# Token projection of a decoder step on one core: the memory's part moved from last to second, and the tokens put back tile by tile

## The reference, cut to what matters

```python
IN_WIDTHS = (NSA_H * HD, 3 * NSA_H, 2 * NSA_G * HD, 2 * NSA_G * HD, 2 * NSA_G * HD,
             ML_W, ML_W, ML_H, ML_H, MEM_W, N_BRANCH * D_MODEL)
...
def split_proj(x, norm_mix, w_in):
    offs = [int(o) for o in np.cumsum(IN_WIDTHS)[:-1]]
    return jnp.split(rmsnorm(x, norm_mix) @ w_in, offs, axis=-1)
```

## Time and profile before

| | |
|---|---|
| Median of 3 runs | 2784.66 us |
| Lowest and highest | 2782.76 and 2791.83 us |
| The profiled execution: its own time | 2783.64 us |
| The profiled execution: its span, first to last instruction | 2782.0 us |
| Mean granted clock of TensorE | 0.939 of full |
| TensorE busy | 2494.7 us, 90% of the span |
| VectorE, ScalarE, GpSimd busy | 1226.7, 807.5, 226.0 us |

### The profile page before, as it was taken

One profiled execution on the slowest core, in us unless ns is written; L12 is line 12 of the kernel. 1 busy time (PEld: TensorE's weight loads), 2 busy tenths in 40 slices (PEclk: granted clock), 3 DMA queues, 4 the chain that ended last, 5 costly groups with the idle time before them and its releaser, 6 DMA issues. The chain is left out here.

```text
span 2782.0 us, 40213 instructions
## 1 busy us (share of the span) xinstructions
PE 2494.7 (90%) x15394; PEld 2203.1 (79%) x15394; DVE 1226.7 (44%) x2361; ACT 807.5 (29%) x1765; POOL 226.0 (8%) x310
## 2 busy tenths in 40 slices
PE   6977798799666899987978999998799999999999
PEld 6965588799565677764448999996699999999997
DVE  4546566222536766645553233323423333333334
ACT  4253264443333444432223121112221111111110
POOL 1003221030100000014420000000000000000000
PEclk9978599899798999988889999999899999999999
DMA  4011431312110000016622111113121111111111
GB/s 145 16 31 34 125 101 54 122 48 71 60 33 1 1 1 1 1 47 170 157 69 57 46 46 46 46 35 122 46 61 46 46 46 46 46 46 46 46 31 61
DMA packets 206218, 156.75 MB, mean 56 GB/s; under 512 B 68354, under 2 KB 187189, under 8 KB 205972
## 3 DMA queue, kind: packets, MB, share of 16 engines
q1 hardware_dynamic: 180804, 124.15, 15.4%
q0 software_dynamic: 8096, 18.98, 2.5%
q10 hardware_dynamic: 17136, 11.12, 1.4%
HBM read 142.76 MB, written 15.59 MB: 57 GB/s over the span
## 5 line engine op out<-in xcount | busy, mean ns | idle before, releaser
L177 PE MATMUL ps<-brT_r,ff_wih 128*128 128x344 f32 x1056 | 338.0, 320 | 11.0 <-DVE ff_wi_r L165 11.0
L179 PE MATMUL ps<-brT_r,ff_wi_r 128*128 128x344 f32 x1056 | 337.5, 320 | 0.0
L178 PE MATMUL ps<-xnT_r,ff_wih 128*128 128x344 f32 x1056 | 337.4, 319 | 0.0
L177 PEld LDWEIGHTS ps<-brT_r,ff_wih 128*128 128x128 f32 x1056 | 199.2, 189 | 12.2 <-DVE ff_wi_r L165 11.1
L179 PEld LDWEIGHTS ps<-brT_r,ff_wi_r 128*128 128x128 f32 x1056 | 198.9, 188 | 0.0
L178 PEld LDWEIGHTS ps<-xnT_r,ff_wih 128*128 128x128 f32 x1056 | 198.6, 188 | 0.4
L3415 ACT ACTIVATE ff_sa<-ps 128x344 f32<-128x344 f32 x66 | 30.3, 459 | 578.0 <-PE ps L179 578.0
L177 PE MATMUL ps<-x_r,mg_wh 128*128 128x344 f32 x576 | 184.8, 321 | 11.3 <-DVE mg_w_r L165 11.3
L179 PE MATMUL ps<-x_r,mg_w_r 128*128 128x344 f32 x576 | 184.3, 320 | 0.0
L178 PE MATMUL ps<-xnT_r,mg_wh 128*128 128x344 f32 x576 | 184.3, 320 | 0.0
L3451 DVE TENSOR_TENSOR x<-x,ps 128x512 f32<-128x512 f32 (+1 forms) x198 | 134.9, 685 | 104.3 <-PE ps L179 103.5
(11 more groups left out here) (556 smaller groups left out, 5687.3 us busy)
## 6 DMA issues: line engine op xcount, KB each, us to landing
ff_wi<-in_w_ffn_in SPq DMA_DIRECT2D x44, 512.0 KB, 5.1
mg_w<-in_w_in SPq DMA_DIRECT2D x24, 512.0 KB, 4.1
ff_wo<-in_w_ffn_out SPq DMA_DIRECT2D x11, 1024.0 KB, 4.9
s_pages<-in_cache_kv_slc POOLq DMA_DIRECT2D x128, 64.0 KB, 2.8
s_pages<-in_cache_kv_slc SPq DMA_DIRECT2D x128, 64.0 KB, 2.8
sc_X<-in_cache_kv_cmp SPq DMA_DIRECT2D x56, 128.0 KB
sc_X<-in_cache_kv_cmp POOLq DMA_DIRECT2D x56, 128.0 KB, 2.4
x<-in_w_in SPq DMA_DIRECT2D x6, 1024.0 KB, 6.0
```

The source lines that it names most:

```text
L177: nc.tensor.matmul(out, wh, xh, start=(first and k == 0), stop=False)
L178: nc.tensor.matmul(out, wh, xl, start=False, stop=False)
L179: ins = nc.tensor.matmul(out, wl, xh, start=False, stop=(last and k == n - 1))
```

## The change

The groups of the projection stand in another order: gates and raw rows (0), the four groups of the memory (1 to 4), memory queries (5, 6), queries (7, 8), all keys (9), all values (10).

- The memory's weights are no longer in the two slots of `x2`. Groups 1, 2 and 3 are loaded at the start of the stage into `kvsw`, `q` and `mq`, which are not yet written then, and group 4 into `kvsw` when group 1 is done. Each is loaded by two DMAs of 128 columns, in runs of 512 bytes.
- The memory's results stay in PSUM banks 4 to 7 until all four groups are done; ACT then copies them out in four copies. They go to `memh`, the place of the memory's high parts. The token groups now go round four banks instead of six.
- Keys and values are two groups by kind, so their weights are gathered by four DMAs each in runs of 256 bytes.
- The tokens are restored by tile while the last group runs (`restore`), with the norming and rotation of the keys between.
- In the stage ahead, the first group's weights are loaded early into a free buffer `X_[:, 1]` and split in two halves, the second half and a part of tile 0 behind `norm`; SP then loads one group's weights there instead of two.
- `p_` of the cross-attention lies in rows of `brT`.

The diff, cut to what the change is made of:

```diff
+TOK_N = (280,) + (256,) * 10
+TOK_X = (0, 5, 6, 7, 8, 9, 10)
...
-    return M["I"]["w_in"].rearrange("(k p) n -> p k n", p=P)[:, :, C_MQ + g * 256:C_MQ + (g + 1) * 256]
-def tok_weights(M, g, part, n=256):
+    col = (C_G, C_MQ)[g]
+    return M["I"]["w_in"].rearrange("(k p) n -> p k n", p=P)[:, :, col:col + TOK_N[TOK_X[g]]]
...
-    groups = [(wv, C_MQ + o, 256, mq, o) for o in (0, 256)]
-    groups += [(wv, C_Q + o, 256, q, o) for o in (0, 256)]
-    groups += [(wv, C_G, 280, gk, 0)]
-    groups += [(wv, C_KVS + o, 256, kvsw, o) for o in (0, 256)]
-    NX = len(groups)
-    groups += [(mv, o, 256, kvm, o) for o in (0, 256, 512, 768)]
-    NGR = len(groups)
...
+    NGR, MEM = len(TOK_N), (1, 2, 3, 4)
+    GATES, MQ, Q, KK, KV = 0, (5, 6), (7, 8), 9, 10
...
+    def weights(g, part):
+        if g in TOK_X:
+            return tok_weights(M, TOK_X.index(g), part, TOK_N[g])
+        name = ("kvsw", "q", "mq", "kvsw")[g - 1]
+        flat = A[name if part == "raw" else name + "R"][:, :, :].rearrange("p t n -> p (t n)")
+        at = KT * 256 * (part == "hi")
+        return flat[:, at:at + KT * 256].rearrange("p (k n) -> p k n", k=KT)
...
+        mem_bank = lambda c_, t: 4 + 2 * c_ + t
...
+        splits = {(0, 0): 1, (0, 1): 2, (0, 2): 3, (0, 3): 5, (2, 1): 4, (3, 1): 6, (6, 1): 7, (7, 1): 8, (8, 1): 9,
+                  (9, 1): 10}
+        split_no = {g: i + 1 for i, g in enumerate(splits.values())}
+        roots = {(5, 2): at_mk, (7, 3): at_mq, (9, 3): at_q, (10, 1): at_k}
...
+                def load_mem_w(g):
+                    for h in range(2):
+                        sp.dma_start(weights(g, "raw")[:, :, h * XD:(h + 1) * XD],
+                                     mv[:, :, 2 * ((g - 1) % 2) + h, (g - 1) // 2, :]).then_inc(in_m[g - 1], 16)
+                for g in (1, 2, 3):
+                    load_mem_w(g)
...
+                for g in TOK_X[2:]:
+                    i = TOK_X.index(g)
+                    sp.wait_ge(projected, last[TOK_X[i - 2]] + 1)
+                    if g in (KK, KV):
+                        for r in range(4):
+                            sp.dma_start(weights(g, "raw")[:, :, r * HD:(r + 1) * HD], kvv[:, :, r, g - KK, :]
+                                         ).then_inc(in_w[i % 2], 16)
+                    else:
+                        col = {MQ[1]: C_MQ + 256, Q[0]: C_Q, Q[1]: C_Q + 256}[g]
+                        sp.dma_start(weights(g, "raw"), wv[:, :, col:col + 256]).then_inc(in_w[i % 2], 16)
+                    if g == MQ[1]:
+                        sp.wait_ge(projected, last[1] + 1)
+                        load_mem_w(4)
...
+                        sp.wait_ge(kept, xlast[GATES] + 1)
...
+                    if g == Q[0]:
+                        sp.dma_start(O["win_sample"][:, 0:WIN - 1].rearrange("b w g c d -> b w (g c d)"),
...
                 sp.wait_ge(kready, 1)
+                sp.wait_ge(kept, xlast[KV] + 1)
...
+                    if g in TOK_X:
+                        if nx >= 4:
+                            pe.wait_ge(kept, nx - 3)
+                        if g == 0 and t in starts:
+                            pe.wait_ge(x_low, 2 * starts.index(t) + 1)
+                        dst = ps[0:m, nx % 4, 0:w]
+                        x = lambda k: (xh(k)[:, rows], xnR[:, k, rows])
+                        nx += 1
+                    else:
+                        if g == MEM[0]:
+                            pe.wait_ge(m_low, 1)
+                        col = (g - 1) % 2 * 256
+                        dst = ps[:, mem_bank((g - 1) // 2, t), col:col + 256]
...
+                    if i == 0:
+                        continue
...
+                    if (g, t) in splits:
+                        split_w(splits[(g, t)])
+                    if (g, t) == (2, 1):
+                        for tt in range(2):
+                            for h in range(XH):
+                                square(ps[:, mem_bank(0, tt), h * XD:(h + 1) * XD], XD, 144 + tt * XH + h)
+                    if (g, t) == (4, 1):
+                        for cc in range(2):
+                            for tt in range(2):
+                                nc.scalar.activation(kvm5[:, tt, :, cc, :], ps[:, mem_bank(cc, tt), :].rearrange(
+                                    "p (h d) -> p h d", h=XH), ACT.Copy).then_inc(mkept, 1)
...
+                for g in (1, 2, 3, 5, 4, 6):
                     split_w(g)
-                    if g == 3:
-                        mean(at_mq, XD, 1)
-                        root(at_mq, 1)
-                    if g == 5:
-                        mean(at_q, HD, 3)
-                        root(at_q, 2)
-                        dve.wait_ge(in_g, 80)
-                        chain.link(dve, nc.vector.tensor_tensor(q4, q4, bc(by_head(at_q, H), 3, HD), ALU.mult))
-                        chain.link(dve, nc.vector.tensor_tensor(q4, q4, gb(gq, H), ALU.mult))
-                dve.wait_ge(projected, last[NX - 1] + 1)
-                whole(nc, xnT[:, 0:4, :], xnR[:, 0:4, :], brR[:, 0:4, :]).then_inc(restored, 1)
-                split_w(NX + 1)
-                whole(nc, xnT[:, 4:8, :], xnR[:, 4:8, :], brR[:, 8:12, :]).then_inc(restored, 1)
-                mean(at_k, HD, 6)
-                split_w(NX + 2)
-                root(at_k, 3)
+                mean(at_mk, XD, squared, 2 * XH)
+                root(at_mk, 1)
+                dve.wait_ge(mkept, 4)
+                dve.wait_ge(in_g, 80)
+                chain.link(dve, nc.vector.tensor_tensor(km4, km4, bc(by_head(at_mk, XH), 3, XD), ALU.mult))
+                nc.vector.tensor_tensor(km4, km4, bc(bc(gmk, 1, XH), 1, 2), ALU.mult).then_inc(mready, 1)
+                split_w(7)
+                mean(at_mq, XD, kept, xlast[MQ[1]] + 1)
+                split_w(8)
+                root(at_mq, 2)
+                split_w(9)
+                mean(at_q, HD, kept, xlast[Q[1]] + 1)
+                split_w(10)
...
+                def restore(t):
+                    rows = slice(t * P, (t + 1) * P) if t < QT else slice(S, T)
+                    dve.wait_ge(projected, first[KV] + t + 1)
+                    for k, kb in ((0, 0), (4, 8)):
+                        whole(nc, xnT[:, k:k + 4, rows], xnR[:, k:k + 4, rows], brR[:, kb:kb + 4, rows]
+                              ).then_inc(restored, 1)
...
+                for t in range(4, TT):
+                    restore(t)
...
-        p_ = st.sb("p", [P, 2, XH, XT])
+        p_ = brT[:, 0:2, :].rearrange("p a t -> p (a t)")[:, 0:2 * XH * XT].rearrange("p (b h n) -> p b h n", b=2, h=XH)
...
-        A["kvm"] = brT[:, 0:2, :].rearrange("p a t -> p (a t)")[:, 0:2048].rearrange("p (t n) -> p t n", t=2)
...
+            kvm, A["memh"] = s2.pair("memh", [P, KT, XT])
+            A["kvm"] = kvm[:, :, :].rearrange("p k t -> p (k t)").rearrange("p (t n) -> p t n", t=2)
...
+        first = X_[:, 1, 0:KT * TOK_N[0]].rearrange("p (k n) -> p k n", k=KT)
+        next_w = lambda part, k: tok_weights(M, 0, part, TOK_N[0])[:, k:k + 4, :]
+        x_in, x_hi, x_lo = M["xnT"][:, 4:8, 0:P], M["brR"][:, 8:12, 0:P], M["xnR"][:, 4:8, 0:P]
...
+                sp.wait_ge(turned, NF * (B - 1))
+                sp.dma_start(first, tok_group(M, 0)).then_inc(M["tok_in"], 16)
...
-                for g in range(2):
-                    sp.dma_start(tok_weights(M, g, "raw"), tok_group(M, g)).then_inc(M["tok_in"], 16)
+                sp.dma_start(tok_weights(M, 1, "raw"), tok_group(M, 1)).then_inc(M["tok_in1"], 16)
...
-                act.wait_ge(M["tok_in"], 16 * 2)
-                high(nc, tok_weights(M, 0, "hi"), tok_weights(M, 0, "raw")).then_inc(M["tok_high"], 1)
+                act.wait_ge(M["tok_in"], 16)
+                for k in (0, 4):
+                    high(nc, next_w("hi", k), first[:, k:k + 4, :]).then_inc(M["tok_high"], 1)
+                high(nc, x_hi, x_in).then_inc(M["tok_high"], 1)
...
+                def next_low(k):
+                    dve.wait_ge(M["tok_high"], k // 4 + 1)
+                    low(nc, next_w("lo", k), first[:, k:k + 4, :], next_w("hi", k)).then_inc(tok_low, 1)
...
+                    if n == 1:
+                        next_low(0)
...
+                dve.wait_ge(M["tok_high"], 3)
+                low(nc, x_lo, x_in, x_hi).then_inc(tok_low, 1)
                 keep_k(EARLY // 4)
-                dve.wait_ge(M["tok_high"], 1)
-                low(nc, tok_weights(M, 0, "lo"), tok_weights(M, 0, "raw"), tok_weights(M, 0, "hi")).then_inc(tok_low, 1)
-                dve.wait_ge(tok_low, 1)
```

## The result

| | before | changed |
|---|---|---|
| Median of 4 runs | 2785.64 us | 2756.06 us |
| Lowest and highest | 2782.76 and 2791.83 us | 2749.59 and 2757.96 us |
| The profiled execution | 2783.64 us | 2749.59 us |
| Ratio of the runs | | 0.9887, 95% interval 0.9863 to 0.9910 |

So 1.1% faster. The forecast was 2751, the range 2744.5 to 2761. The profiled executions differ by 34.0 us, but 3.4 of it arise ahead of that place: SP issues the first spill of the compressed keys at 481.41 instead of 484.79.

What follows compares the result with a forecast made beforehand. TensorE's waits and slow stretches, mainly for weights in the projection, were taken as the bound. Gains of 6.7 (A) + 25.2 - 0.3 (B) + 1.2 (C) = 32.8 us, off 2783.64, gave 2751 us, range 2744.5 to 2761.

Steps and rivals of the forecast that it cites:

- Part A: Projection's start: values' spill lands earlier behind 1 MB less of weights, TensorE starts at 496.7 instead of 503.4; gain 6.7 us.
- Part B: Memory groups: weights there in time, no eviction between, 22.3 us instead of 47.5; gain 25.2 us, less 0.3 for group 4.
- the forecast margin: Memory group 4: its low part ends at G+16.1, TensorE wants it at G+16.7, so 0.6 us to spare.
- the rival by the runs of 256 bytes: Gathered weights of keys and values land late and stop TensorE; slower than before, 2784 to 2792 us; chance 0.03.
- Part C: Projection's end: key norming moved to the middle, SP's four issues now last, 4.0 us idle instead of 5.21; gain 1.2 us.
- Rival 1: Cross-attention starts at full clock because the clock holds through the 4 us wait; 2748.5 us; chance 0.15.

Runs made afterwards that it cites:

- start undone: Changed kernel with both loads of next-stage weights at their old place, first group split whole behind keep_k, tile 0 split in two parts again: 2763.32 us, ratio 0.9928.
- group 4 late: Changed kernel with the load of the fourth memory group issued one memory group (5.6 us) later: 2762.04 us, ratio 0.9919.
- no staging: Changed kernel with the memory's weights in the two slots of x2 as before, split behind tile 1 of the group ahead: 2781.92 us, ratio 0.9993.
- rotation later: Changed kernel with GpSimd's rotation of the queries and its sample-row transfer moved to the stage behind the cross-attention: 2750.27 us, ratio 0.9876.
- load behind spills: Changed kernel with the remaining 1 MB load to x issued behind both spills, not ahead of the values' spill: 2755.57 us, ratio 0.9893.
- copy of keys earlier: Changed kernel with VectorE's three added low parts reordered, first behind the norm's two products, others behind keep_k: 2754.79 us, ratio 0.9897.

## Why the prediction was right

**Part A, 6.7 forecast, 6.3 measured.** The reason held: the values' spill ends the stage, by GpSimd's start in the changed kernel and by the run that moves the load. Sizes: it lands 9.4 us after the first spill's issue instead of 12.0, so 2.6 us earlier, not 3.1 for 1 MB at 334 GB/s. DVE's tail ended 6.9 us after the first spill's issue, 0.7 later than forecast, for a reason I had not seen: the first low part did not only fill DVE's idle time, it doubled GpSimd's root, from 1.01 to 2.01 us. The values' spill covered this: with the root back at 1.01 us nothing is won.

**Part B, 24.9 forecast, 24.9 measured.** The four groups took 22.5 us, no wait was left, group 4 had the forecast margin, and the gathered weights landed in 7.5 us of the 21.3 they may take, so the rival by the runs of 256 bytes was far off. Without staging 27.4 us are lost, of which 17.5 are waits.

**Part C, 1.2 forecast, 0.8 measured.** SP's issues took 3.04 us as before; what the forecast had too short was the time around them, 0.49 ahead and 0.86 behind against its 0.45 and 0.5. DVE ended 0.3 us after TensorE, forecast 0.5.

**The cross-attention, no change forecast, 2.4 us lost.** Rival 1, to which I had given 0.15, came to pass in its result and not in its mechanism: the first scores ran at full clock and 2.25 us were won, but the clock had not held through the wait. It fell, the transposes paid for it as before, and it was back earlier. The step that failed was that a stage whose code is the same keeps its length, and that a gain at its start stays. The scores arrived while GpSimd rotated, and what that cost, 1.7 us of wait and 1.4 of slower matmuls behind it, was more than the 2.25. Only the 1.7 us are shown to be GpSimd's by the run that moves its rotation; that the longer wait brought the slow stretch behind it is likely and not shown. The remaining 1.5 us are a stretch at half clock at the stage's end, with a cause that stays open.

**The distance to 2751.** The sum was made against an execution of 2783.64, the medians against 2785.64: 2.0. The three terms were 0.8 too large, the cross-attention lost 2.4: 2750.8 + 5.2 = 2756.0, where 2756.06 was measured. That it agrees so well is luck, since single executions lie 8 us apart.

## What to carry to other kernels

When groups of work are shorter than the chain load, high, low, put their operands in place ahead of them, in any rows not yet written; the order alone brought nothing here. Before shifting a stage in time, look at what stands on GpSimd at that place: VectorE's short operations beside it can cost more than the shift brings, here 1.7 us of wait, or 3.1 with the slow matmuls behind it, against 2.25. At a stage's end count the issues of the queue that must wait for the last result, and ask which of them the next stage could make.

## What was not expected of the hardware

- **VectorE and GpSimd run one after the other, not side by side, for some operations.** A VectorE operation on four columns took 1.23 us beside GpSimd and 0.17 alone; a product 2.29 against 1.23; a GpSimd root 2.01 beside VectorE's low part and 1.01 alone. The recorded durations contain the waiting, and no idle time shows it. The reduction from PSUM took 1.23 us in both cases. The Trainium skill, "SBUF — State Buffer", section "SBUF: two separate sides", says that the two share a pair of ports as an exclusive lock, held by whichever starts first for the whole instruction. On VectorE's side it concerns operations in a two-port mode, and those with two SBUF inputs where GpSimd's reads SBUF too. The product and the low part have two SBUF inputs, and for them the trace agrees, in the ends of the rows too. The column of four numbers has one; it was held up as well, and no row tells its mode.
- **The clock behind a wait was not the same each time.** After 4.4 us without a matmul, behind 150 us or more of gapless work, the clock fell to half in all eight executions, and the transposes took 1.82 to 1.94 us. In six (changed twice, start undone, group 4 late, no staging, rotation later) it was full again for the first scores, which took 1.97 us; in two (load behind spills, copy of keys earlier) it was not, and they took 3.75 and 3.70. After 0.7 us the transposes took 1.07 us and the scores 1.97 each time, after 9.2 us the scores took 3.75. What decides between the six and the two stays open.
